# Expert items of 96 slots in place of 128 in the mixture-of-experts stage of a decoder step

## The reference, cut to what matters

```
logits = t @ w_router                       # t: 288 x 1024, 8 experts
top_logits, top_idx = top_k(logits, 2)
gates = softmax(top_logits)
combine = sum(one_hot(top_idx, 8) * gates)
for e in range(8):                          # w_gate, w_up: 1024 x 3584; w_down: 3584 x 1024
    out += combine[:, e] * ((silu(t @ w_gate[e]) * (t @ w_up[e])) @ w_down[e])
```

## Time and profile before

| | |
|---|---|
| three runs | 1490.03, 1491.48 and 1492.24 us, median 1491.48 |
| span of the profiled execution | 1489.5 us; its own time is not listed apart, and the median lies 2.0 us above its span |
| PE, PEld, DVE, ACT, POOL busy | 1476.5, 1258.8, 1196.2, 975.1, 162.4 us |
| first expert product, last expert product | 532.7 us, 1481.9 us |
| granted TensorE clock | 1.000 over the span |
| moved | 456.64 MB, mean 307 GB/s |

### The profile page before, as it was taken

One profiled execution on the slowest core, in us unless ns is written; L12 is line 12 of the kernel. 1 busy time (PEld: TensorE's weight loads), 2 busy tenths in 40 slices (PEclk: granted clock), 3 DMA queues, 4 the chain that ended last, 5 costly groups with the idle time before them and its releaser, 6 DMA issues.

```text
span 1489.5 us, 21413 instructions
## 1 busy us (share of the span) xinstructions
PE 1476.5 (99%) x8116; PEld 1258.8 (85%) x8116; DVE 1196.2 (80%) x1088; ACT 975.1 (65%) x933; POOL 162.4 (11%) x159
## 2 busy tenths in 40 slices
PE   8999999999999999999999999999999999999998
PEld 6987699999988978888888888888888888888887
DVE  5698576665556688888888888888889888888987
ACT  5444464443455587777777777777777778777775
POOL 3653000000000048200001001001000000000100
PEclk9999999999999999999999999999999999999999
DMA  7562983427554379999999999999999999999990
GB/s 256 194 260 71 391 307 114 170 100 253 186 186 155 111 258 390 362 395 383 394 393 382 396 393 382 394 395 382 393 394 360 394 393 370 386 390 362 371 366 32
DMA packets 196822, 456.64 MB, mean 307 GB/s; under 512 B 9988, under 2 KB 13102, under 8 KB 196762
## 3 DMA queue, kind: packets, MB, share of 16 engines
q1 hardware_dynamic: 188912, 439.60, 79.6%
q0 software_dynamic: 4336, 13.15, 3.1%
q10 hardware_dynamic: 3514, 3.08, 0.7%
HBM read 443.78 MB, written 12.03 MB: 306 GB/s over the span
## 4 chain that ended last, share of the span: by engine, by line
PE 94%; DVE 2%; ACT 1%; SPq 1%; issue 1%; DMA 1%; DVEq 0%; ACTq 0%
PE bank L2041 25%; PE bank L2570 13%; PE bank L2572 13%; PE bank L2571 13%; PE bank L2584 7%; PE bank L2586 7%; PE bank L2585 7%; PE bank L2594 2%; PE bank L2246 1%; DMA ring<-in_attn_w_in 1%; PE bank L2258 1%; PE bank L2220 1%; PE bank L2339 0%; DVE wql L1827 0%; SPq L686 0%
## 5 line engine op out<-in xcount | busy, mean ns | idle before, releaser
L1827 DVE TENSOR_TENSOR wql<-ring,wqh 128x2048 fp32r<-128x2048 f32 x335 | 766.8, 2291 | 107.3 <-ACT wqh L994 106.5
L994 ACT ACTIVATE wqh<-ring 128x2048 fp32r<-128x2048 f32 x334 | 641.5, 1921 | 230.8 <-PE bank L2572 148.4
L2570 PE MATMUL bank<-wqh,xgh 128*128 128x512 f32 x892 | 353.7, 396 | 0.2 <-DVE wql L1827 0.2
L2571 PE MATMUL bank<-wql,xgh 128*128 128x512 f32 x896 | 349.2, 390 | 0.0
L2572 PE MATMUL bank<-wqh,xgl 128*128 128x512 f32 x892 | 348.0, 390 | 0.0
L2572 PEld LDWEIGHTS bank<-wqh,xgl 128*128 128x128 f32 x892 | 167.5, 188 | 35.9
L2570 PEld LDWEIGHTS bank<-wqh,xgh 128*128 128x128 f32 x892 | 167.5, 188 | 34.4 <-DVE wql L1827 1.0
L2571 PEld LDWEIGHTS bank<-wql,xgh 128*128 128x128 f32 x896 | 168.5, 188 | 32.9
L994 ACT ACTIVATE wd<-ring 128x1024 fp32r<-128x1024 f32 x90 | 95.1, 1059 | 133.4 <-PE bank L2041 133.4
L2584 PE MATMUL bank<-wqh,heTh 128*128 128x512 f32 x440 | 171.4, 389 | 0.0
L2586 PE MATMUL bank<-wqh,heTl 128*128 128x512 f32 x440 | 171.2, 389 | 0.0
(11 more groups left out here) (457 smaller groups left out, 1962.6 us busy)
## 6 DMA issues: line engine op xcount, KB each, us to landing
ring<-in_moe_w_gate SPq DMA_DIRECT2D x56, 2048.0 KB, 15.2
ring<-in_moe_w_up SPq DMA_DIRECT2D x56, 2048.0 KB, 15.1
ring<-in_moe_w_down SPq DMA_DIRECT2D x56, 2048.0 KB, 15.2
ring<-in_attn_w_in SPq DMA_DIRECT2D x6, 2048.0 KB, 15.8
ring<-in_ffn_w_gate SPq DMA_DIRECT2D x5, 2048.0 KB, 16.3
ring<-in_ffn_w_up SPq DMA_DIRECT2D x5, 2048.0 KB, 10.9
ring<-in_cache_k SPq DMA_DIRECT2D x16, 512.0 KB, 6.5
ring<-in_cache_v SPq DMA_DIRECT2D x16, 512.0 KB, 5.7
```

The source lines that it names most:

```text
L994: return nc.scalar.activation(dst, src, ACT.Copy)
L1827: return v.tensor_tensor(dst, src, head.bitcast(F32), ALU.subtract)
L2570: mm(bank, xgh[:, k, :], w_h[:, part], start=(k == 0), stop=False)
L2571: mm(bank, xgh[:, k, :], w_l[:, part], start=False, stop=False)
```

## The change

The slot count of an item, 128 so far as `P`, becomes `SL = 96`. Each array of slots in a product, transpose, copy or transfer of the expert stage is cut to 96. The turned blocks keep their places, one every 128 columns, and are reached through `slots_in`, as four pieces of 96. The bounds that decide on further items become 96 and 192 rows; the largest number of items stays 24.

```diff
+SL = 96
-MAXBLK = (T + P - 1) // P
+MAXBLK = (T + SL - 1) // SL
...
+    def slots_in(t):
+
+        return t[:].rearrange("p (k s) -> p k s", k=4)[:, :, 0:SL]
...
-            pool.indirect_dma_start(out=xgr[:], out_offset=None, in_=x_rows,
-                                    in_offset=bass.IndirectOffsetOnAxis(ap=slots_from[:, 0:1], axis=0)).then_inc(xg_in, 16)
+            pool.indirect_dma_start(out=xgr[0:SL, :], out_offset=None, in_=x_rows,
+                                    in_offset=bass.IndirectOffsetOnAxis(ap=slots_from[0:SL, 0:1], axis=0)).then_inc(xg_in, 16)
...
         def silu(i, c):
-            nc.scalar.activation(he[:], banks[c % NCH % 2][:], ACT.Silu).then_inc(sg_ok, 1)
+            nc.scalar.activation(he[0:SL, :], banks[c % NCH % 2][0:SL, :], ACT.Silu).then_inc(sg_ok, 1)
...
-            copy(dst, banks[6][:]).then_inc(heTh_ok, 1)
+            copy(dst, slots_in(banks[6])).then_inc(heTh_ok, 1)
...
-        v.tensor_scalar(r8[0:1, 2, 5:6], r8[0:1, 2, 4:5], float(P), float(E), ALU.is_gt, ALU.mult)
-        v.tensor_scalar(r8[0:1, 2, 6:7], r8[0:1, 2, 4:5], float(2 * P), float(E), ALU.is_gt, ALU.mult).then_inc(many, 1)
+        v.tensor_scalar(r8[0:1, 2, 5:6], r8[0:1, 2, 4:5], float(SL), float(E), ALU.is_gt, ALU.mult)
+        v.tensor_scalar(r8[0:1, 2, 6:7], r8[0:1, 2, 4:5], float(2 * SL), float(E), ALU.is_gt, ALU.mult).then_inc(many, 1)
...
-            v.tensor_tensor(he[:], he[:], banks[2 + c % NCH % 2][:], ALU.mult).then_inc(he_ok, 1)
+            v.tensor_tensor(he[0:SL, :], he[0:SL, :], banks[2 + c % NCH % 2][0:SL, :], ALU.mult).then_inc(he_ok, 1)
...
-            minus(low, banks[6][:], high).then_inc(heT_ok, 1)
+            minus(slots_in(low), slots_in(banks[6]), slots_in(high)).then_inc(heT_ok, 1)
...
-                    last = mm(bank[:, P * j:P * j + P], rows[:, P * c:P * c + P], pick[:, m, :],
+                    last = mm(bank[:, P * j:P * j + SL], rows[:, P * c:P * c + P], pick[:, m, 0:SL],
...
-                last = tr(bank[:, P * j:P * j + P], xgr[:, P * c:P * c + P], ident[:])
+                last = tr(bank[:, P * j:P * j + SL], xgr[0:SL, P * c:P * c + P], ident[0:SL, 0:SL])
...
-                bank = banks[2 * kind + c % NCH % 2][:]
+                bank = banks[2 * kind + c % NCH % 2][0:SL, :]
...
-                    mm(bank, xgh[:, k, :], w_h[:, part], start=(k == 0), stop=False)
-                    mm(bank, xgh[:, k, :], w_l[:, part], start=False, stop=False)
-                    last = mm(bank, xgl[:, k, :], w_h[:, part], start=False, stop=(k == KD - 1))
+                    mm(bank, xgh[:, k, 0:SL], w_h[:, part], start=(k == 0), stop=False)
+                    mm(bank, xgh[:, k, 0:SL], w_l[:, part], start=False, stop=False)
+                    last = mm(bank, xgl[:, k, 0:SL], w_h[:, part], start=False, stop=(k == KD - 1))
...
-                    left = slice(P * (2 * h + j), P * (2 * h + j) + P)
+                    left = slice(P * (2 * h + j), P * (2 * h + j) + SL)
...
-                last = tr(banks[6][:, P * j:P * j + P], he[:, P * j:P * j + P], ident[:])
+                last = tr(banks[6][:, P * j:P * j + SL], he[0:SL, P * j:P * j + P], ident[0:SL, 0:SL])
```

More of the change, by code:

```diff
@@ L1345, in take_gathered @@
         def take_gathered(bank, half):
-            return copy(xgh[:, 4 * half:4 * half + 4, :], bank[:].rearrange("p (k s) -> p k s", k=4)).then_inc(xgh_ok, 1)
+            return copy(xgh[:, 4 * half:4 * half + 4, 0:SL], slots_in(bank)).then_inc(xgh_ok, 1)
         def silu(i, c):
-            nc.scalar.activation(he[:], banks[c % NCH % 2][:], ACT.Silu).then_inc(sg_ok, 1)
+            nc.scalar.activation(he[0:SL, :], banks[c % NCH % 2][0:SL, :], ACT.Silu).then_inc(sg_ok, 1)
         def take_heT(i, c, dst):
             act.wait_ge(t_full, i * NCH + (c + 1))
-            copy(dst, banks[6][:]).then_inc(heTh_ok, 1)
+            copy(dst, slots_in(banks[6])).then_inc(heTh_ok, 1)
         act.wait_ge(*B.full("rt"))
@@ L1381, in act_body @@
                 if last and p == halves - 1:
-                    take_heT(i, NCH - 1, heTh2)
+                    take_heT(i, NCH - 1, slots_in(heTh2))
                 head(i, HPRO + p)
@@ L1387, in act_body @@
                     if c < NCH - 1 or not last:
-                        take_heT(i, c, heTh[:])
+                        take_heT(i, c, slots_in(heTh))
                         act.wait_ge(*after_half(i, place(GATE, c + 1)))
@@ L1410, in act_body @@
                 if last:
-                    copy(ysbh[:, part], banks[4 + half][:]).then_inc(yh_ok, 1)
+                    copy(ysbh[0:SL, part], banks[4 + half][0:SL, :]).then_inc(yh_ok, 1)
                 else:
-                    nc.scalar.activation(ysb[:, part], banks[4 + half][:], ACT.Copy,
-                                         scale=slots_to[:, 1:2].bitcast(F32))\
+                    nc.scalar.activation(ysb[0:SL, part], banks[4 + half][0:SL, :], ACT.Copy,
+                                         scale=slots_to[0:SL, 1:2].bitcast(F32))\
                         .then_inc(y_out, 1)
@@ L1903, in picks @@
                     dve.wait_ge(dup_ok, 1)
-                last = v.tensor_scalar(pick[:, m, :], iota[:], slot_of[:, m, bass.ds(item, 1)], None, ALU.is_equal)
+                last = v.tensor_scalar(pick[:, m, 0:SL], iota[:, 0:SL], slot_of[:, m, bass.ds(item, 1)], None, ALU.is_equal)
             return last
@@ L1974, in dve_body @@
                     if c < NCH - 1 or not last:
-                        heT_tails(i, c, heTl[:], heTh[:])
+                        heT_tails(i, c, heTl, heTh)
                 if p % 6 == 0 and p >= 6 and not ends:
@@ L1986, in dve_body @@
                 dve.wait_ge(yh_ok, half + 1)
-                minus(ysbl[:, part], banks[4 + half][:], ysbh[:, part]).then_inc(y_ok, 1)
+                minus(ysbl[0:SL, part], banks[4 + half][0:SL, :], ysbh[0:SL, part]).then_inc(y_ok, 1)
         GA_BANK = [banks[7], banks[1]]
@@ L2550, in scatter @@
             m, half = k % 2, k // 2
-            part, left = slice(CH * half, CH * half + CH), pickT[:, P * m:P * m + P]
-            mm(bank[:], left, ysbh[:, part], start=True, stop=False)
-            mm(bank[:], left, ysbl[:, part], start=False, stop=True).then_inc(sc_full, 1)
+            part, left = slice(CH * half, CH * half + CH), pickT[0:SL, P * m:P * m + P]
+            mm(bank[:], left, ysbh[0:SL, part], start=True, stop=False)
+            mm(bank[:], left, ysbl[0:SL, part], start=False, stop=True).then_inc(sc_full, 1)
         def scatter_samples(half, bank):
-            part, left = slice(CH * half, CH * half + CH), pickT[:, NP + NS * (1 - half):NP + NS * (1 - half) + 2 * NS]
-            mm(bank[0:2 * NS, :], left, ysbh[:, part], start=(half == 0), stop=False)
-            return mm(bank[0:2 * NS, :], left, ysbl[:, part], start=False, stop=(half == 1))
+            part, left = slice(CH * half, CH * half + CH), pickT[0:SL, NP + NS * (1 - half):NP + NS * (1 - half) + 2 * NS]
+            mm(bank[0:2 * NS, :], left, ysbh[0:SL, part], start=(half == 0), stop=False)
+            return mm(bank[0:2 * NS, :], left, ysbl[0:SL, part], start=False, stop=(half == 1))
         def half_tile(i, n, kind, c, last_item=False):
@@ L2636, in pe_body @@
                         r = ROWS[m]
-                        piece = tr(banks[7][:, P * m:P * m + r], pick[0:r, m, :].bitcast(F32), ident[0:r, 0:r])
+                        piece = tr(banks[7][0:SL, P * m:P * m + r], pick[0:r, m, 0:SL].bitcast(F32), ident[0:r, 0:r])
                     piece.then_inc(pg_full, 1)
```

34 lines of the change are left out of this document (17 added, 17 removed).

## The result

The changed kernel takes 1496.1 us (median of six runs, 1494.3 to 1496.7), the kernel before 1490.8 (six runs on the same chip, 1490.0 to 1492.2): the ratio is 1.0032, with an interval of 1.0021 to 1.0044. It is 5.3 us slower. Forecast were 1484.0 us, and faster with a chance of 0.70: the direction was wrong, the range missed, and the case "slower", at 0.13, came true, but not by the mechanism that stood there for it.

What follows compares the result with a forecast made beforehand. PE, busy 99% of the span, was taken as the bound. Transposes gave -7.5 us and all else 0, so the 1489.5 us span became 1482.0, plus 2.0 for the median: 1484.0 us, range 1480 to 1493.

Steps and rivals of the forecast that it cites:

- the case "slower": Whole kernel: slower by more than about 0.2% (3 us), through Rival 3 with its neighbours; chance 0.13.
- Stationary width does not enter the distance: 4032 expert products: 96 stationary columns for 128 leave starts 0.227 us apart, the shorter load being hidden; 0 us.
- The bound of +6 us: Expert products: if 64 columns' slowness came from width, 96 would have half, 4032 x 1.5 ns, 6 us more.
- the merged row: Groups of four transposes: sign of being right, their joint length falls from 0.60 to 0.52 us or less.
- The sum of 7.5 us: 280 transposes: 96 moving columns for 128 save 26.7 ns each, 7.5 us in all.
- Rival 2: Transposes: no faster, still 0.109 us apart, held by the 128-column load or a fixed cost; 1491.5 us, chance 0.16.
- The gather: 40 products gathering item 0, ahead of the first item: 96 moving columns gain at most 1.1 us; taken as 0.
- The covers: Expert stage: ACT, DVE and weight transfers keep up with PE; 385 GB/s asked for at most, 394 delivered before.
- Smaller copies, silu and transfers: ACT, DVE and POOL: less work, all beside PE's stream; 0, from -1 us to 0 for ACT and DVE.
- Rival 1: Expert products: load width counts, 13.8 us less beside the transposes' 7.5; 1470.2 us, chance 0.07.
- Rival 3: 63 transpose groups: PE drains where array shape changes, 0.18 us each, 11.4 us more; 1495.4 us, chance 0.13.
- Rival 4: Expert stage: an expert with over 96 rows makes eight more items run; 2433 us, chance 0.01.

Runs made afterwards that it cites:

- experiment 2: Kernel before with only its expert products at 96 stationary columns; transposes, copies, slots and transfers stay at 128: 1501.2 us, ratio 1.0071.
- experiment 7: Changed kernel with only the gather of item 0 (40 products and their choice matrix) at 128 moving columns again: 1493.4 us.
- experiment 3: Kernel before with only its expert products at 64 stationary columns: 1500.4 us, ratio 1.0067.
- experiment 1: Kernel before with only its transposes at 96 moving columns: 1485.0 us, ratio 0.9962.
- experiment 8: Changed kernel with products, copies of the turned blocks and gather at 128 columns again; transposes, silu, slots and transfers stay at 96: 1484.7 us, ratio 0.9957.
- experiment 13: Kernel before with one product in twelve (336 in all) at 96 stationary columns, the other 3696 at 128: 1503.4 us, ratio 1.0084.

## Why the prediction was wrong

The account of the 5.3 us, from the runs: products +10.6 (experiment 2); transposes -7.2 beside narrow products (from the start of the product ahead of a group of four to that of the second behind it pass 0.799 us, 0.901 in experiment 2, and 56 x 0.102 is 5.7; each of the seven groups of eight takes 0.213 less, 1.5 in all); the clock in the gather +2.7. These make +6.1; the 0.8 between that and 5.3 is within the spread of the medians, and nothing here tells it from zero. With the 7.8 us between experiments 2 and 7 in place of the 7.2, the sum is +5.5.

**The products: the failed step.** "Stationary width does not enter the distance. I take 0." It enters with 2.7 ns each at 96 columns, 4032 x 2.7 = 10.9 us. The bound of +6 us, from the products of 64 columns, was on the right side and too small. The step went wrong in how it read its rows. In the earlier trace rows the distances of 64 columns, 0.24 and 0.23, were longer than 0.227, as are those of experiment 3 (0.230), and I put them down to their place. The earlier trace rows are of another kind, products of plain 32-bit numbers with 288 moving columns, and the rule that held there (0.241 at 128 and at 72 columns) does not carry over. And the load being hidden, with idle time to spare, was taken to mean that its width can't matter. The idle time of the loader rose in every narrow version, and the products went slower: cover by idle time is not a proof that the hidden instruction is without effect on the pace.

**The transposes**: the distance fell from 109 to 83 ns, as worked out, and the merged row is 0.49 us where 0.52 or less was named. The sum of 7.5 us was too large by a quarter with wide products: experiment 1 has 5.6. The term was mis-sized there, since a group of four has three inner distances and one of eight has seven: 56 x 0.076 + 7 x 0.182 = 5.5 us. In the changed kernel it came to 7.2 us, near the forecast, but that is luck: the rest is not in the group. From the first to the second product behind it pass 0.291 us with both the transposes and the products at 96, and 0.314 to 0.318 with only one of them or none (experiments 1 and 2, kernel before). Why is open. Rival 2 is refuted.

**The gather**: taken as 0, bounded at 1.1 us of gain. It cost 2.7 us by the clock, which no step of mine looked at. At full clock the 0 would have been right, as the distances of 111 to 112 ns show. The fall stands in the windows, and experiment 7 ties it to the 96 moving columns of the gather. The Trainium skill, "TensorE: Matmul & The Clock Gate", section "What's actually happening", describes a clock that depends on PE's recent activity; the trace agrees in that the clock fell (1.00 to 0.52) while only the moving columns were fewer.

**The covers held.** From 700 to 1400 us ACT waited 180.5 us for PE in place of 171.8 and DVE 87.5 for ACT in place of 79.6, and PE for them once in the expert stage, 0.4 us; 391 and 373 GB/s were moved for what PE asked. Smaller copies, silu and transfers were taken as 0, and experiment 8 beside experiment 1 shows no difference beyond the spread.

**The rivals.** Rival 1, a faster product by a narrower load, has the wrong sign. Rival 3 gave 1495.4 us and the kernel came to 1496.1, but it is wrong all the same: from the last product to the first transpose pass 909.35 - 909.12 = 0.23 us, not 0.32, and the groups became shorter. That its time fits is chance; without the starts one would have taken it for shown. Rival 4, twice the items, did not occur: 8116 matmuls as before.

**Still open** is why a width has the pace it has. A load of w columns and a matmul that fills w rows of the bank always changed together in these runs, so they are not told apart, and the means by place in experiment 13 describe the disturbance without explaining it.

## What to carry to other kernels

Before a hidden load is made narrower, measure the distance between starts in a long stream at exactly the new width: here 128 columns of rounded 32-bit numbers are the fastest of nine widths, 127 costs 1.5% of the kernel, and a single narrow product in twelve costs more than making all narrow. Shrink the moving side (the transposes) and leave the stationary side full, even if part of it is never read. After a change that shortens many matmuls in a row, read the granted clock window by window around them, since the whole run's mean (0.998) hardly shows a fall of 7 us.

## What was not expected of the hardware

The load's time goes straight with its columns: 188, 174, 161 and 134 ns for 128, 112, 96 and 64, some 0.84 ns a column. The Trainium skill, page "TensorE: Matmul & The Clock Gate", section "LDWEIGHTS", has such a slope, and the trace agrees in the slope alone: by its formula 128 columns take 107 ns, and the load measured here has 188. The distance, which that load should leave alone, does not follow it.

At 96 columns the distances in the changed kernel repeat in fours, 229, 231, 231 and 229 ns behind some groups of transposes, 229, 231, 232 and 228 behind others, while equal products of 128 columns stay at 226 or 227. A group of transposes disturbs that stream too, for up to ten products (235, 231, 233, 227, 229, 231 from the second distance on, by mean over all groups), and it finds its pace again; behind a narrow product in experiment 13 it had not done so within twelve, where the next narrow one came.
